# A first modulation chunk issued in two halves, six cache pages ahead of it, and twelve products of ones at the start of TensorE

## The reference

```
(s_m, a_m, g_m, s_f, a_f, g_f) = silu(c) @ W_ada + b_ada      (per sequence; 9 sequences, 6 x 1024 outputs)
h = RMSNorm(x) * (1 + a_m) + s_m
p = h @ W_in
A = latent attention; keys of the 8 samples come from a paged cache:
    k_nope = c_kv @ W_uk, k = RMSNorm([k_nope, k_rope]) * g_qk_k   (8 samples x 8 pages of 128 positions)
B = short convolution branch, C = chunked spatial gate branch
x = x + g_m * W_o(sig(gA)*A + sig(gB)*B + sig(gC)*C)
x = x + g_f * MoE(RMSNorm(x) * (1 + a_f) + s_f)               64 experts, top-8, one shared
```

## Time and profile before

| | us |
|---|---|
| median of 3 runs | 1010.48 (1009.39 to 1010.88) |
| the profiled execution, its own time | 1010.36 |
| its span, first to last instruction | 1008.6 |
| PE busy | 972.6 (96%) |
| DVE busy | 610.6 (61%) |
| ACT busy | 188.0 (19%) |
| DMA, mean over the span | 309 GB/s |

### The profile page before, as it was taken

How to read it: one execution, slowest core, us unless ns; L and a number is a source line. 1 busy time by engine, 2 the same in 40 slices (tenths; PEclk the granted TensorE clock), 3 DMA queues, 4 the chain that set the end, 5 groups by cost and what they waited for, 6 DMA issues and landing times.

```text
span 1008.6 us, 14072 instructions
## 1 busy us (share of the span) xinstructions
PE 972.6 (96%) x4542; PEld 547.3 (54%) x4542; DVE 610.6 (61%) x1563; ACT 188.0 (19%) x385; POOL 56.6 (6%) x81
## 2 busy tenths in 40 slices
PE   6999999999999999999999999999999999999997
PEld 2487766444447788888744344444444444344443
DVE  3513322468754011123749889889888888888875
ACT  3311231335435100002510010000000000000000
POOL 0100010000000000000210000000000000000000
PEclk9999999999999999999999999999999999999999
DMA  8994469655545483544569999999999999999991
GB/s 314 421 402 186 175 228 322 180 164 169 162 125 235 160 356 132 209 159 176 214 244 415 425 424 424 426 421 419 423 428 422 422 427 420 425 422 421 422 393 61
DMA packets 54921, 311.86 MB, mean 309 GB/s; under 512 B 8922, under 2 KB 28410, under 8 KB 32978
## 3 DMA queue, kind: packets, MB, share of 16 engines
q1 hardware_dynamic: 48546, 297.21, 74.0%
q0 software_dynamic: 6320, 13.93, 3.9%
HBM read 315.80 MB, written 3.95 MB: 317 GB/s over the span
## 4 chain that ended last, share of the span: by engine, by line
PE 73%; DMA 20%; DVE 3%; issue 1%; SPq 1%; ACT 0%; DVEq 0%; PEldq 0%
PE bank L747 48%; DMA ring<-in_w_e_gu 18%; PE pA L747 17%; PE pB L747 4%; PE pC L747 3%; DMA pT<-in_poolT 1%; PE pD L747 1%; PE pA L782 1%; DMA ring<-in_w_br 0%; PE pA L991 0%; SPq L592 0%; DVE xT L2327 0%; PE pC L1000 0%; PE bank L1315 0%; DVE xT L2403 0%
## 5 line engine op out<-in xcount | busy, mean ns | idle before, releaser
L747 PE MATMUL pA<-ring,qT 128*64 128x512 f32 x992 | 226.8, 595 | 11.1 <-DMA ring<-in_w_e_gu 11.0
L2315 DVE STREAM_TRANSPOSE qT<-xs 32x256 f32<-32x256 f32 x480 | 209.2, 436 | 7.7
L747 PE MATMUL bank<-hT,ring 128*128 128x264 f32 (+1 forms) x832 | 189.3, 388 | 0.9 <-PE bank L747 0.9
L747 PEld LDWEIGHTS bank<-hT,ring 128*128 128x128 f32 (+1 forms) x832 | 154.3, 189 | 34.4 <-issue 8.7
L747 PEld LDWEIGHTS pA<-ring,qT 128*64 128x64 f32 x992 | 74.0, 137 | 137.7 <-issue 128.8
L747 PE MATMUL bank<-pT,vtok 128*128 128x264 f32 x512 | 127.9, 393 | 0.3 <-DVE pT L2407 0.3
L747 PEld LDWEIGHTS bank<-pT,vtok 128*128 128x128 f32 x512 | 92.0, 190 | 39.3 <-issue 26.7
L2324 DVE TENSOR_TENSOR pT<-pT,bank 128x264 f32<-128x264 f32 x248 | 99.9, 427 | 8.8 <-PE bank L747 7.3
L747 PE MATMUL bank<-wuk,ring 128*128 128x512 f32 x192 | 86.3, 597 | 0.0
L747 PE MATMUL pB<-ring,oaT 128*64 128x512 f32 x244 | 62.0, 605 | 0.0
L747 PE MATMUL pC<-ring,oaT 128*64 128x512 f32 x244 | 60.3, 592 | 0.0
(11 more groups left out here) (344 smaller groups left out, 795.0 us busy)
## 6 DMA issues: line engine op xcount, KB each, us to landing
ring<-in_w_e_gu SPq DMA_DIRECT2D x62, 2048.0 KB, 18.9
ring<-in_w_e_dn SPq DMA_DIRECT2D x61, 1024.0 KB, 18.6
ring<-in_poolT SPq DMA_DIRECT2D x64, 208.0 KB, 2.7
ring<-in_w_ada SPq DMA_DIRECT2D x12, 1024.0 KB, 9.6
ring<-in_w_bg SPq DMA_DIRECT2D x4, 3072.0 KB, 11.6
ring<-in_w_mix SPq DMA_DIRECT2D x5, 2048.0 KB, 8.7
ring<-in_w_ada SPq DMA_DIRECT2D x4, 2048.0 KB, 12.5
ring<-in_poolR SPq DMA_DIRECT2D x56, 128.0 KB, 2.1
```

Source lines behind the costliest of these rows:

```text
L747: return nc.tensor.matmul(out, lhsT, rhs, start=start, stop=stop)
L2315: last = V.transpose(xTs[32 * j:32 * j + 32, q % 2, :, 32 * a:32 * a + 32], src[32 * a:32 * a + 32, j])
```

## The change

Of W_ada's first chunk (slot 0) the half with the first four row tiles is issued right behind wuk, ahead of the wait for the page table, and counts on the semaphore of the first page group; the other half is issued after pages 0 to 5. The pages are grouped anew (`EGROUP`), and which bank a page's product takes is now told by its own list `EBANK`, cut where other products stand between the pages. On SP pages 4 and 5 move ahead of the chunk, xT and vec, and page groups and chunks 1 to 3 alternate otherwise. On PE pages 0 to 5 come ahead of the first chunk, and 12 products of `ones` with itself into pD come first of all, behind the third constant of POOL. ACT and DVE take pages 0 to 5 ahead of their part of the chunk and of the norm.

```diff
-EGROUP = (0, 1, 4, 6, 8, 10, 12, 16)
+EGROUP = (0, 1, 2, 4, 6, 8, 12, 16)
+EBANK = (0, 4, 6, 8, 10, 12)
...
-STAGES = [("ek0", 1), ("ek1", 3), ("ada0", 1), ("ek4", 2), ("ek6", 2), ("norm1", 1), ("ada1", 1), ("ek8", 2), ("ada2", 1),
+STAGES = [("ek0", 4), ("ek4", 2), ("ada0", 1), ("ek6", 2), ("norm1", 1), ("ada1", 1), ("ek8", 2), ("ada2", 1),
...
 def early_bank(e):
-    g = max(x for x in EGROUP if x <= e)
+    g = max(x for x in EBANK if x <= e)
...
             def ada_item(x):
+                if x == 0:
+                    sp.dma_start(part(0, CT * 512, CT, 512), A["w_ada"][0][:, CT:DT]).then_inc(wgt[0], 16)
+                    return
                 if x < 4:
...
             sp.dma_start(wuk, A["w_uk"]).then_inc(d_early[0], 16)
+            sp.dma_start(part(0, 0, CT, 512), A["w_ada"][0][:, 0:CT]).then_inc(d_early[0], 16)
             sp.wait_ge(d_ptab, 16)
-            early_pages(0)
-            early_pages(1)
+            for g in range(4):
+                early_pages(g)
             ada_item(0)
             sp.dma_start(xT[:], A["xT"]).then_inc(d_in, 16)
             sp.dma_start(vec[:], A["vec"]).then_inc(d_in, 16)
-            early_pages(2)
-            early_pages(3)
+            early_pages(4)
             ada_item(1)
-            early_pages(4)
+            early_pages(5)
             ada_item(2)
-            early_pages(5)
             early_pages(6)
             ada_item(3)
...
-                        pe.wait_ge(d_early[g], 16 * (EGROUP[g + 1] - e + (g == 0)))
+                        pe.wait_ge(d_early[g], 16 * (EGROUP[g + 1] - e + 2 * (g == 0)))
...
-            early_keys(0, 2)
-            early_keys(2, 4)
+            pe.wait_ge(s["consts"], 3)
+            for _ in range(12):
+                mm(pD[:, 0:P], ones[:], ones[:], True, True)
+            early_keys(0, 6)
             pe.wait_ge(s["csilu"], 1)
             pe.wait_ge(d_late, 16)
             ada_item(0)
-            early_keys(4, 6)
             pe.wait_ge(s["consts"], 6)
             early_keys(6, 8)
             colsum("norm1", rstd[:], 1)
...
-            early_squares(0, 4)
+            early_squares(0, 6)
             ada_rows((0,))
             act.wait_ge(d_in, 16 * 2)
             nc.scalar.activation(sq[:], xT[:], ACT.Square).then_inc(s["sq1"], 1)
-            early_squares(4, 8)
+            early_squares(6, 8)
...
-            early_sums(0, 4)
+            early_sums(0, 6)
             dve.wait_ge(s["sq1"], 1)
             tile_sums(rstd[:], sq[:])
-            early_sums(4, 8)
+            early_sums(6, 8)
```

## The result

The changed kernel takes 1011.98 us (median of 20 runs, 1010.47 to 1014.14) against 1009.82 of the kernel before in the same sessions (20 runs, 1009.14 to 1013.89): a ratio of 1.0018, 95% interval 1.0011 to 1.0025. A second comparison, in a later session, gave 1.0023, interval 1.0014 to 1.0033. So it is slower, by about 0.2%, just where, by the prediction's own figure, a measurement of this kernel begins to tell a difference from none.

A forecast was written before the change was run, and what follows sets the result against it. TensorE was taken as the bound, with start delays reaching the end: +1.3 us by the norm's chain, or +2.6 with the clock down, the latter on the 1010.48 median giving 1013.1 us; range 1010.4 to 1014.8.

The forecast's parts named there:

- Page 0 behind a half chunk: Start of PE: page 0 also waits for 1024 KB of w_ada, so PE starts 2.5 us later, at 8.2.
- T: Time at which PE begins page 0; taken as 8.2 us, bounds 7.4 and 8.6, against 5.74 before.
- The ones: Start of PE: twelve products run from 2.4 to 7.7, cost nothing and save 1.75 us of slow first products.
- The sum: Whole kernel: +1.3 us by the norm's chain, or +2.6 with the clock down, giving 1013.1 from a median of 1010.48.
- (b): Start of PE: ones don't raise the clock, or it drops before page 0; up to 1.75 us more, 1013.5 to 1014.8; chance 0.15.
- What becomes late: First norm: the side chain ends at 27.1, PE waits 2.7 us for it; the norm's reading moves 1.3 us later.
- The clock: New wait before the column sum: clock falls to 1.2 GHz, costing 1.45 us on PE's own way, bounds 0 and 1.75.
- PE's own way: PE from column sum to the fold: 1.15 us later, or 2.6 with 1.45 for the low clock.
- the norm's chain: From the norm's reading of the column sum, 5.8 us of steps gate the fold; +1.3 us.
- (a): New wait before the column sum: clock stays up over the 2.7 us; +1.3 us, 1011.8; chance 0.27.
- (c): Start: half chunk lands at the full rate, page 0 at 7.4; 0.8 us less, 1012.3 with the clock down; chance 0.08.
- (d): Expert stage: the start is lost in later waits and the end doesn't move; 1010.5; chance 0.10.

The follow-up runs named there:

- known delay: Kernel before plus 48 products of ones between page 15 and the first projection; ratio 1.0112 (1.0097 to 1.0127), 11.3 us.
- The first experiment: Changed kernel with ACT squaring xT behind page 4, ahead of the chunk's copy; 1008.64 us, ratio 0.9982 to the kernel before.
- The second: Changed kernel with twelve more products of ones on PE between page 7 and the column sum; ratio 1.0008 to the kernel before.
- the version with xT early: Changed kernel with page 0 waiting for wuk and itself, half chunk behind page 3, seven ones, side chain behind page 3; 1007.77 us, ratio 0.9984.
- the half chunk behind page 2: Against the version with xT early: first half of the chunk issued behind page 2 instead of page 3, pages regrouped; ratio 0.9998 to the kernel before.
- the whole chunk: Changed kernel with the first modulation chunk issued whole behind pages 0 to 5; ratio 1.0008 to the kernel before.

## Why the prediction was right, and where it was off

*Page 0 behind a half chunk.* T was put at 8.2, between 7.4 and 8.6; it was 8.10, and 8.2 to 8.5 in the other executions with the half chunk ahead. The half chunk landed 5.6 us after its issue at 2.06, page 0 4.4 after 3.64. The line through two landing times on an idle queue was good to 0.3 us.

*The ones.* They took 4.88 us and ended 0.76 before page 0, so they cost nothing; the pages ran at the high clock. Their worth was mis-sized: 1.75 us by the first page of the kernel before, 2.4 without them here, and 3.0 by the four pages in the execution with the known delay. The point at which the clock rises varies, and one execution was too little to price it from. The sum does not suffer from it, as it takes the pages at the high clock; rival (b) does.

*Pages, chunk, transfers behind them.* Chunk at 18.60 (18.5 foretold), page 6 without a wait for its transfer, nothing behind them late. The chunk's time is luck in a small part: six pages take 10.50 from first product to chunk and not 10.3, and T was 0.1 early.

*What becomes late.* The wait of 2.7 us was 2.70, column sum at 27.23 (27.1), DVE's reading of it at 28.59 (28.4). The first experiment shows the cause: with the square of xT ahead of the copy, the wait is gone and so is the loss. The second splits it: with the wait filled, the fold is 1.35 us nearer to page 0, and what is left of the loss goes with the side chain.

*The clock.* 1.45 us were put down for it on PE's own way, which is 1.3 at the fold (2.6 less the 1.3 by the norm's chain). At the fold the filled wait shows 1.35. On PE's own way it was 1.6: from the column sum to the fold PE takes 8.35 us, and 6.74 in the version with xT early, where it runs the same list at the high clock and waits for no other engine. The clock had fallen 0.2 us before the column sum and not 0.5, so more of the low stage fell on work. The fall came inside the wait in one profiled execution and just behind it in another, and cost nearly the same. The fold was foretold for 35.5 and was at 35.58. The Trainium skill, TensorE: Matmul & The Clock Gate, in Part 1 on the HAM clock gate, says that the point at which the clock rises is not tied to the kernel's start and shifts from run to run. The rows agree: the same 24 matmuls of ones took between 4.54 and 5.49 us in five profiled executions. They show the same of the fall, 2.5 us after the last matmul in one execution and 3.5 in the other. The section on HAM oscillation that the prediction cites from the same page of the Trainium skill describes longer waits than this one, so it backed the forecast less than the prediction says; what carried it is the row with the fall at 2.2 us.

*The sum.* +2.6 us was forecast; the fold is 2.71 later, and the first routed expert product, 516.18 before, starts at 518.87, 2.69 later. The profiled spans, 1008.6 and 1010.4, differ by only 1.8. The missing 0.9 is in the expert stage: from its first product to the end it took 492.4 us before and 491.5 after. Nothing shows it to be a gain of the change. That stage took between 490.7 and 493.2 in the profiled executions of this study, in no order of when it began (490.7 for the earliest start, 514.82, 493.2 for the next, 515.33, and 491.5 for the latest, 527.97), and the known delay came through whole. PE waits in it for single expert transfers of 22 to 24 us: 14 times, 11.0 us in all, in the profiled execution of before, and 12 times, 10.0 us, in that of the change, which accounts for the missing 0.9. The two ratios, 1.0018 and 1.0023, are 1.8 and 2.3 us; the forecast's 2.6 lies just above the first interval (1.1 to 2.5 us) and inside the second (1.4 to 3.3). The chance of over 0.2% was put at one half, and the time came out on that line. The time itself, 1011.98, is 1.1 us under the 1013.1 of the sum: 0.66 of it is that 1010.48, from three runs, stood for the kernel before, which had 1009.82 in twenty. By that time alone rival (a), 1011.8, would fit better than the forecast; as a difference of the medians, +2.16, it lies between the +1.3 of (a) and the +2.6. It is the windows, the fold and the filled wait that tell the two apart.

*Rivals.* (a), the clock stays up over the wait: not in the two profiled executions, but a wait of 2.85 us in the version with the half chunk behind page 2 left it up, so it was a real chance. (b), the ones don't raise the clock: no. Its price was too low: without the ones the ratio was 1.0062, and its upper bound, 1014.8, is 1.0043 of 1010.48. (c): no, T was 8.1. (d), the start is lost later: no, by the known delay.

## What to carry to other kernels

When work is moved ahead on the engine that is the bound, look at what another engine has queued behind the moved work: here a chain of 6 us on ScalarE and VectorE, hidden behind four pages of matmuls, had only two left to hide it, and it needed nothing from the chunk but its place in the list. Move such a chain with, or ahead of, the thing it waits behind. And price a wait on TensorE with the low clock that may follow it: here 2.7 us of waiting brought 1.35 more.

## What the runs showed of the hardware

The granted clock did not fall after a fixed idle time. It fell 2.5 us after the last matmul in the changed kernel. Behind the same wait of 2.70 us it fell 0.8 us after work had begun again in the second execution, and 0.4 us after (at 30.1) in the one without the ones. With the whole chunk it fell after two shorter waits, 1.15 and 1.89 us, when PE had been back at work for 1.4 us, since 26.70:

```profile
27.00:28.00 1.00, 1.00 (x10) 0.66 (x12) 1.00 (x3) 0.00 (x0) 0.00 (x0) 1.00 0.92 393
28.00:29.00 1.00, 1.00 (x8) 0.22 (x4) 0.85 (x2) 0.00 (x0) 0.00 (x0) 0.53 1.08 459
```

And it did not fall in or behind the 2.85 us before the chunk with the half chunk behind page 2:

```profile
18.00:19.00 1.00, 0.00 (x0) 0.00 (x0) 0.00 (x0) 1.00 (x1) 0.00 (x0) 1.00 1.33 550
19.00:20.00 1.00, 0.00 (x0) 0.00 (x0) 0.17 (x1) 1.00 (x2) 0.00 (x0) 1.00 0.91 387
20.00:24.00 4.00, 3.19 (x19) 1.17 (x20) 3.85 (x1) 1.48 (x3) 0.00 (x0) 1.00 0.98 398
```

A low clock behind a wait can thus be read in one trace and be missing in the next. The record of the granted clock also reads 1.00 over the first 12 us of every profiled execution, although the 24 matmuls of ones in the changed kernel take 4.88 us, 0.20 each, and the 96 of the known delay 0.11 each; there the spacing has to be read.
